# A two-layer transformer with a gated second block: the second norm's division moved behind the feed-forward part, first columns turned during the second half of the output products, two attention hand-overs moved

## The reference

```
for l in range(2):
    h = rms_norm(x, norm1[l]);  proj = h @ w_in[l]
    o_a, o_b, o_c, o_d = latent, sliding-window, top-k and forget-gate attention, 4 heads each
    x = x + concat(o_a, o_b, o_c, o_d) @ w_out[l]            # 1024 x 1024
    h2 = rms_norm(x, norm2[l])
    x = x + square(relu(h2 @ w_up[l])) @ w_down[l]           # 1024 x 4096, 4096 x 1024
return rms_norm(x, final_norm)

def rms_norm(x, g):
    y = x * rsqrt(mean(x * x, axis=-1) + EPS)
    return y * g
```

## Time and profile before

| what | value |
|---|---|
| runs | 2093.21, 2099.13, 2101.03 us, median 2099.13 us |
| profiled execution: time, span | 2098.79 us, 2096.9 us |
| TensorE busy | 2017.5 us, 96% |
| VectorE busy | 1116.5 us, 53% |
| ScalarE busy | 837.0 us, 40% |
| mean granted clock of TensorE | 0.983 |

### The profile page before, as it was taken

The page is one execution under the profiler, slowest core; times in us unless marked ns, Lnnn a source line. Parts: engine busy times, 40 slices in busy tenths (PEclk is TensorE's granted clock), DMA queues, the critical chain, the costliest instruction groups (busy, mean ns, idle before and its releaser), DMA issues. The chain is left out here.

```text
span 2096.9 us, 27760 instructions
## 1 busy us (share of the span) xinstructions
PE 2017.5 (96%) x10624; PEld 1624.0 (77%) x10628; DVE 1116.5 (53%) x2039; ACT 837.0 (40%) x1744; POOL 359.8 (17%) x345
## 2 busy tenths in 40 slices
PE   8999999999999999999999999799999998999997
PEld 7776578888887877567888888688877897886676
DVE  5788634423434489734552553578866331425655
ACT  4444633322323344653331332444443333534632
POOL 1335710000000153650000000003030330003300
PEclk9999999999999999899999999999999999999999
DMA  6331022332332432002552433133224323341232
GB/s 185 85 92 51 1 71 91 98 103 85 96 121 67 123 102 78 11 31 81 178 174 93 169 116 117 51 121 90 82 69 139 83 69 97 100 133 49 73 128 80
DMA packets 177525, 198.30 MB, mean 95 GB/s; under 512 B 38755, under 2 KB 140786, under 8 KB 176882
## 3 DMA queue, kind: packets, MB, share of 16 engines
q1 hardware_dynamic: 177394, 196.53, 30.4%
HBM read 180.74 MB, written 11.55 MB: 92 GB/s over the span
## 5 line engine op out<-in xcount | busy, mean ns | idle before, releaser
L161 DVE TENSOR_TENSOR weight_pairs<-weight_ring,weight_pairs 128x1024 fp32r<-128x1024 f32 (+4 forms) x293 | 355.1, 1214 | 413.5 <-ACT weight_pairs L152 413.0
L182 PE MATMUL psum<-operand,weight_pairs 128*128 128x512 f32 x1320 | 527.1, 399 | 13.4 <-PEq L230 11.3
L152 ACT ACTIVATE weight_pairs<-weight_ring 128x1024 fp32r<-128x1024 f32 (+4 forms) x293 | 303.3, 1038 | 542.1 <-PE psum L184 522.9
L183 PE MATMUL psum<-operand,weight_pairs 128*128 128x512 f32 x1320 | 517.6, 392 | 0.0
L184 PE MATMUL psum<-operand,weight_pairs 128*128 128x512 f32 x1320 | 517.2, 392 | 0.0
L182 PEld LDWEIGHTS psum<-operand,weight_pairs 128*128 128x128 f32 x1320 | 249.4, 189 | 73.6 <-issue 20.2
L184 PEld LDWEIGHTS psum<-operand,weight_pairs 128*128 128x128 f32 x1320 | 249.0, 189 | 53.8
L183 PEld LDWEIGHTS psum<-operand,weight_pairs 128*128 128x128 f32 x1320 | 249.3, 189 | 51.0 <-issue 1.0
L890 POOL TENSOR_SCALAR probs<-probs,stats 128x128 f32<-128x128 f32 (+3 forms) x176 | 161.4, 933 | 246.1 <-DVE stats L796 245.8
L182 PE MATMUL psum<-weight_pairs,hidden 128*128 128x512 f32 x512 | 200.5, 392 | 0.0
L184 PE MATMUL psum<-weight_pairs,hidden 128*128 128x512 f32 x512 | 199.5, 390 | 0.0
(11 more groups left out here) (417 smaller groups left out, 2724.5 us busy)
## 6 DMA issues: line engine op xcount, KB each, us to landing
weight_ring<-in_w_in_dram SPq DMA_DIRECT2D x100, 512.0 KB, 3.7
weight_ring<-in_w_up_dram SPq DMA_DIRECT2D x64, 512.0 KB, 3.6
weight_ring<-in_w_down_dram SPq DMA_DIRECT2D x64, 512.0 KB, 3.6
weight_ring<-in_w_out_dram SPq DMA_DIRECT2D x24, 512.0 KB, 3.5
ada_rows<-in_ada_w_dram SPq DMA_DIRECT2D x24, 512.0 KB, 4.6
spilled<-v_t SPq DMA_DIRECT2D x22, 256.0 KB, 4.2
weight_ring<-in_w_in_dram SPq DMA_DIRECT2D x20, 256.0 KB, 2.9
weight_ring<-in_w_proj_a_dram SPq DMA_DIRECT2D x8, 512.0 KB, 3.4
```

Of the source, the lines that this page charges most:

```text
L152: act.activation(self.pairs[:, i % SPLIT_RING, 0, 0:n], self.buf[:, i % RING, 0:n], ACT.Copy).then_inc(self.rounded, 1)
L161: dve.tensor_tensor(self.pairs[:, i % SPLIT_RING, 1, 0:n], self.buf[:, i % RING, 0:n], self.pairs[:, i % SPLIT_RING, 0, 0:n].bitcast(F32), ...
L182: pe.matmul(out, lhs[0], rhs[0], start=start, stop=False)
L183: pe.matmul(out, lhs[0], rhs[1], start=False, stop=False)
```

## The change

Four things are different.

1. `OutputProducts` has a tail of its own. It multiplies x with the gain alone, in half rows of 512 columns (`add`), with three slots. The first columns' half rows are transposed while the second half's products run (`turn`: 4 transposes each), three of them after the second half's first weight item. The second columns follow tile by tile, one tile later; the last tile's 4 transposes are given to the up projection (`last_turn`), which makes them after its first 12 matmuls. `keep_busy` is not called in this tail. ScalarE only squares, and at the end VectorE makes `factor` = 1 / (mean + EPS).
2. The feed-forward part's adds (in `mlp`, and `Residual.add` in its tail) multiply the product by `factor` with scalar_tensor_tensor. The up projection waits for its operand in two steps (`ready`): first columns, then all.
3. The mixed heads of chunks 0 to 3 lie in a buffer `mixed`, in place of group a's queries and keys, which lie in a buffer of their own for that.
4. In `attention`, `fill` is called after steps 32, 33 and 34, and VectorE's held-back part comes at step 2. The gain row is loaded when 48 jobs' scores are done, not 16; its transfer is still issued behind the same weights.

```diff
@@ attention
-            if fill is not None and p in (pairs + TURN - 1, pairs + VALUES - 1):
+            if fill is not None and p in range(pairs, pairs + TURN):
                 fill(pe)
...
-            if p == HOLD and held is not None:
+            if p == HOLD + 1 and held is not None:
                 finish_woven(held["dve"])
@@ product_by_channels
+        if ready:
+            pe.wait_ge(*ready[i])
         for h, bank in enumerate(banks):
...
+            if between is not None and (i, h) == (0, 0):
+                between(pe)
@@ OutputProducts
+    def bank(self, c, t):
+        return self.psum[:, 2 + t % 2 if c else t, :].rearrange("p (k c) -> p k c", k=4)
+
+    def turn(self, pe, c, t):
+        n = T * c + t
+        pe.wait_ge(self.scaled, n + 1)
+        if c:
+            pe.wait_ge(self.low_rows, T if t < 2 else T + t - 1)
+        for k in range(4):
+            mm = pe.transpose(self.bank(c, t)[:, k, :], self.scaled_rows[:, n % self.SLOTS, k * P:(k + 1) * P], self.ident[:])
+        mm.then_inc(self.turned, 1)
...
+    def second_half(self, pe):
...
+        for t in range(T - 1):
+            self.turn(pe, 0, t)
...
+            if t:
+                self.turn(pe, 1, t - 1)
+            else:
+                self.turn(pe, 0, T - 1)
...
+    def add(self, dve, c, t):
...
+        dve.tensor_tensor(self.x[:, t, cols], self.psum[:, T * c + t, :], self.x[:, t, cols], ALU.add).then_inc(self.summed, 1)
...
+        dve.wait_ge(self.summed, n + 1)
+        dve.tensor_tensor(self.scaled_rows[:, n % self.SLOTS, :], self.x[:, t, cols], self.gain[:, cols],
+                          ALU.mult).then_inc(self.scaled, 1)
...
         @self.block.scalar
         def _(act):
-            tail.finish_act(act, start, per_half)
+            for i in range(per_half + 1):
+                weights.high(act, start + i)
+            for t in range(T):
+                self.square(act, 0, t)
+            weights.high(act, start + per_half + 1)
+            for t in range(T):
+                self.high(act, 0, t)
+            for t in range(T):
+                self.square(act, 1, t)
+                if t:
+                    self.high(act, 1, t - 1)
+            weights.high(act, end - SPLIT_RING + 1)
+            self.high(act, 1, T - 1)
 
         @self.block.vector
         def _(dve):
-            tail.finish_dve(dve, start, per_half)
+            for i in range(per_half):
+                weights.low(dve, start + i)
+            for t in range(T):
+                self.add(dve, 0, t)
+                if t == T - 2:
+                    weights.low(dve, start + per_half)
+            weights.low(dve, start + per_half + 1)
+            for t in range(T):
+                self.low(dve, 0, t)
+            for t in range(T):
+                self.add(dve, 1, t)
+                if t:
+                    self.low(dve, 1, t - 1)
+            weights.low(dve, end - SPLIT_RING + 1)
+            self.low(dve, 1, T - 1)
+            own = Chain(dve, self.mean_own)
+            dve.wait_ge(self.squared, 2 * T)
+            own(dve.tensor_tensor(self.mean, self.halves[0], self.halves[1], ALU.add))
+            own(dve.tensor_scalar(self.mean, self.mean, 1.0 / D, EPS, ALU.mult, ALU.add))
+            own(dve.reciprocal(self.factor, self.mean))
@@ mlp
-        pe.wait_ge(*input_ready)
-        up_1.products(pe)
+        up_1.products(pe, ((output.low_rows, T), input_ready), output.last_turn)
...
-                dve.tensor_tensor(x[:, t, cols], psum[:, 4 * c + t, :], x[:, t, cols], ALU.add).then_inc(summed_1, 1)
+                dve.scalar_tensor_tensor(out=x[:, t, cols], in0=psum[:, 4 * c + t, :], scalar=output.factor[:, t:t + 1],
+                                         in1=x[:, t, cols], op0=ALU.mult, op1=ALU.add).then_inc(summed_1, 1)
```

More of the change, by code:

```diff
@@ L913, in product_by_tokens, with product_by_channels @@
     return k
-def product_by_channels(pe, psum, banks, weights, pair, chunks, written=None):
+def product_by_channels(pe, psum, banks, weights, pair, chunks, written=None, ready=(), between=None):
     k = 0
@@ L973, in first_half @@
                 for t in range(T):
[L974 to L976 removed]
+                    mm = self.one(pe, t, k, w, kk)
                 k += 1
@@ L980, in first_half, with one @@
                 yield
+    def one(self, pe, bank, k, w, kk):
+        tile = slice((bank % T) * P, (bank % T + 1) * P)
+        return product(pe, self.psum[:, bank, :], [self.lhs[k][:, j, tile] for j in (0, 1)],
+                       [w[j][:, kk, :] for j in (0, 1)], start=(k == 0), stop=(k == KD - 1))
     def fill(self, stored_low, banks_freed):
@@ L1216, in mlp @@
     tail = Residual(psum, x, weights, ident, eps, small, work, operand, sems[:n_tail], again, ident_half)
+    tail.factor = output.factor
     @block.sync
```

126 lines of the change are left out of this document (98 added, 28 removed).

## The result

| kernel | median of the runs | lowest to highest | ratio to before, 95% interval |
|---|---|---|---|
| before | 2099.13 us | 2090.08 to 2102.95 (7) | |
| after | 2108.57 us | 2105.04 to 2111.92 (7) | 1.0054 [1.0035, 1.0072] |

By the medians the changed kernel is 9.4 us (0.45%) slower, by the ratio of the last column, which is not that of the medians, 0.54%. (In the later runs the kernel before had medians of 2095.5 to 2097.5 us, so its 2099.13 is on the high side.) The forecast was 2096.8 us, with a range up to 2101.5: wrong by 11.8 us and on the wrong side. The profiled execution of after has a time of 2109.38 us and a span of 2107.6 us.

The account below looks back on a forecast made before the run. TensorE, busy for 96% of the span, was taken as the bound, with only its pauses and half-clock stretches to win or lose. Terms -2.0-2.4-3.1+3.0+2.2+0.3 = -2.0 us gave 2096.8 us, range 2089.5 to 2101.5.

Parts of the forecast that it names:

- a: Start of attention: VectorE's held-back part one pair later shortens TensorE's pauses before pairs 4 and 5; -2.0 us.
- b: End of attention: first output chunks two steps earlier cover TensorE's pauses before pairs 29 and 30; -2.4 us, both layers.
- c: Output products' tail: after VectorE starts the last tile's add (X), up projection's second item comes 1.55 us earlier; -3.1 us, both layers.
- d: Output products' tail without filling products: 3.9 us pause brings half clock, 1.5 us lost a layer; +3.0 us.
- rival 2: Output products' tail: the pause leaves the clock alone; 2093.8 us, chance 0.13.
- rival 3: Output products' tail: half clock lasts 6.8 us or more, price 3.4 instead of 1.5 us a layer; 2100.6 us, chance 0.14.
- e: Feed-forward tail: ScalarE's square-root table load now falls there, 0.9 us in layer 0, 1.28 in layer 1; +2.2 us.
- f: Feed-forward part: adds become fused multiply and add, 0.06 us more for 4 to 8 of them; +0.3 us.
- Rival 1: Start of attention: the clock stays full; 2090.2 us in both layers, 2093.5 in one; chance 0.25.
- Rival 4: What is won is off the path: a to d bring nothing, e and f stay; 2101.3 us, chance 0.03.

Follow-up runs that it names:

- run 15: Changed kernel with tile distances put back and output tail filled, but the output chunks at the end of attention where they stood before: 2090.98 us, ratio 0.9969 to before.
- run 11: Changed kernel with `small` 96 columns wide, 96 unused bytes ahead of `mixed`, and 60 filling products in the output products' tail: 2092.30 us, ratio 0.9977 to before.
- run 14: As run 11, plus one single-column square root on ScalarE ahead of the feed-forward tail's last four tiles, to load the table there: 2093.03 us, ratio 0.9988 to before.
- run 6: Changed kernel with `small` 96 columns wide instead of 36, tiles behind it 256 bytes further than before the change: 2094.59 us, ratio 0.9995 to before.
- run 8: Second profile of the same kernel as run 6, nothing else changed: 2100.00 us in one run.
- run 12: Changed kernel with `small` 96 columns wide, 96 unused bytes ahead of `mixed`, and VectorE's held-back part one pair earlier again: 2099.93 us, ratio 1.0017 to before.
- run 5: Kernel before with `small` 96 columns wide instead of 32, tiles behind it 256 bytes further: 2094.46 us, ratio 0.9997 to before.
- run 9: Products alone, no kernel: 512 columns at sixteen distances between stationary and moving tile, and bf16 at eight; pitch 226.7 ns at distance 0, 229.0 to 234.2 elsewhere.
- run 13: Products alone again, with eight moving and eight stationary tiles, and with 256 and 384 columns; pitch 226.7 to 226.9 ns at distance 0 with 512 columns.

## Why the prediction was wrong

**The step that failed** is its second sentence: "nearly all the time is matrix products, and the change leaves their number as it is. What can be won or lost are TensorE's pauses and the stretches at half its clock." The number did stay. That their duration would stay as well was taken for granted, and no term, bound or rival was set against it. One line of the change, `small` from 32 to 36 columns, had no part in the sum at all. It cost 1872 products 6.6 ns each, 12.3 us; with it the sum would have been 2096.8 + 12.3 = 2109.1, against 2108.57 measured. That they agree to 0.5 us is luck, as the terms below came out 1.7 to 2.8 us above the forecast's and the median of before is uncertain by some us. Nothing in the profile of before shows this price, as there all tiles read by such products (128x128 by 512 columns) lie at distance 0. But some 69% of the span (6384 products of 226.7 ns) stood on one duration, and an edit that moves the tiles those products read was a reason to bound it.

**Term by term**, for the rest, from the stretches:

- *a*, forecast -2.0: -0.9 a layer over all profiles, -1.8. The pauses changed as forecast: counted from the start of pair 3's scores (179.52 before, 177.80 after), pair 4 starts 2.6 us earlier and pair 5 0.75 us. But the right total came by another way: 0.75 us in layer 0 and 1.3 in layer 1 were to be won by pauses, and most of what shows came from a shorter half clock.
- *b*, forecast -2.4: -0.64 a layer between runs 15 and 11, -1.3. The pauses went, but each of the chunks that are set between pairs takes 0.2 to 0.3 us more than in a row, which I had not counted. The term was mis-sized by nearly a factor of two.
- *c*, forecast -3.1: X to the very first feed-forward add is 138.0 us before and 136.5 in run 11, where no clock is lost: -1.5 a layer, -2.9. Before X, the six sets of transposes cost 0.1 to 0.2 us a layer (24.6 instead of 24.4 and 24.5 us from the first add to X), which takes 0.3 off again. (The forecast's own 96 x 0.23 + 6 x 0.45 us is 24.8, not its 24.6; no term hangs on it.)
- *d*, forecast +3.0: 1.6 and 1.5 us, +3.1. In after rival 2 (no fall) and rival 3 (6.8 us or more) both fell: it was 3.4 us of half clock in each layer. Rival 2 came in no unfilled tail, rival 3 in 3 of 14. The rule cited there from the Trainium skill (TensorE: Matmul & The Clock Gate, "What's actually happening"), that the slow clock is the default and activity lifts it, agrees with run 11, where filling products alone removed it. It doesn't tell of the falls under *What stays open*, in which TensorE was busy.
- *e*, forecast +2.2: 0.9 and 1.2, +2.1, where half clock behind the longer pause lasted 3.4 us. In after it lasted 6.8 us, for which the forecast had nothing, and the term was some +3.2.
- *f*, forecast +0.3: run 14, where a table load no longer stands in the tail, has 356.0 and 367.5 us against 357.4 and 368.9 before. Part c is 1.5 of this, so the fused adds cost 0.1 us a layer, +0.2: each set of four ends 0.2 us later, and some of it is hidden.

This comes to between -0.3 and +0.8 us, where the forecast had -2.0, and run 6, the change without its shift, is 0.05% under before with an interval of 0.17% to either side. Rival 1, a full clock at the start of attention, did not come, but half of it did: in layer 1 of after half clock lasted 3.4 us (from 849.7) instead of 6.8, in layer 0 it stayed 6.8. Rival 4 (nothing on the path) is refuted by the stretches, though the total alone would not have told it from the forecast.

**What stays open.** In four of the profiles (before, runs 6, 8 and 12) the clock falls for 13.7 us in layer 1's attention while TensorE is busy, which costs 6 us; in run 5 it does so in layer 0, in the others not at all, and no edit goes with it. By this luck the profile of after was 6 us better than that of before in this stretch; from the last feed-forward add on it was 7.7 us worse, of which the rows of y are only 2.2, so that the two spans still lie 10.7 us apart, near the 9.4 us of the medians.

**A version that beats both**, by 0.2 to 0.3% of before: run 11 (distances put back, tail filled) at 0.9977 [0.9961, 0.9994] and run 15 at 0.9969 [0.9951, 0.9987]. The two can't be told from each other. All steps together, with the table load ahead and part b kept, are run 14, which has the shortest stretches but a median no better.

## What to carry to other kernels

A tile's size is also the address of every tile behind it. Before a tile is added or widened, look at what remainder by 256 bytes the operands of the long products have, and keep it. When a change makes a kernel slower and no wait has grown, compare the pitch of the same instruction in both traces before looking for a cause in the schedule; and to judge terms of a microsecond, cut the spans at the same events rather than compare medians.

## What the runs showed of the hardware

- In this three-product float32 scheme (fp32r, 128x128 stationary, 512 columns moving) the pitch is 226.7 ns if the stationary and the moving tile are a multiple of 256 bytes apart in the partition, and 229 to 234 ns at the other multiples of 32, the same for both directions of the shift when mirrored (runs 9 and 13). With 384 columns it is 173.3 to 173.4 ns at each of four distances, with 256 columns 118 to 120, and in bf16 with 512 columns 215.8 at each of eight. Why the remainder matters is not shown; that it is no contention with other engines or data transfers is, since in run 9 none works.
- A pause of 3.8 us in TensorE's products was followed by 3.4 us at 1.2 GHz in eleven of 14 tails and by 6.8 us in three; the 3.4 us cost 1.5 to 1.6 us, the 6.8 us 1.1 to 1.3 more; 60 small filling products in its place removed it in all six tails that had them (runs 11, 14 and 15).
- The granted clock also fell for 13.7 us while TensorE was busy throughout, in 5 of 15 profiles, and cost 6 us each time.
